# The first attention's loop over steps is unrolled into pairs on TensorE, VectorE and ScalarE

## The reference

```python
def swa_sink_attention(h, w_qkv, b_qkv, sinks, w_o, b_o):
    qkv = h @ w_qkv + b_qkv
    ...
    q = apply_rope(q, cos[:, None, None], sin[:, None, None]) * (A_HEAD_DIM ** -0.5)
    k = apply_rope(k, cos[:, None], sin[:, None])
    ...
    s = jnp.einsum('bnqkgd,bnskd->bnkgqs', qr, kb).astype(jnp.float32)
    p = sink_softmax(jnp.where(mask[:, None, None], s, NEG_INF), sink).astype(v.dtype)
    o_r = jnp.einsum('bnkgqs,bnskd->bnqkgd', p, vb).reshape(B, n_blk * BLOCK, A_Q_W)
```

## Time and profile before

| | us |
|---|---|
| median of three runs | 3612.8 (3612.68 to 3614.37) |
| the profiled execution | 3607.28 |
| its span | 3605.4 |
| PE busy over the span | 3241.1 (90%) |
| VectorE busy | 1766.6 (49%) |
| ScalarE busy | 1273.1 (35%) |
| GpSimd busy | 1849.1 (51%) |

### The profile page before, as it was taken

One profiled execution on the slowest core, in us unless ns is written; L12 is line 12 of the kernel. 1 busy time (PEld: TensorE's weight loads), 2 busy tenths in 40 slices (PEclk: granted clock), 3 DMA queues, 4 the chain that ended last, 5 costly groups with the idle time before them and its releaser, 6 DMA issues. The chain is left out here.

```text
span 3605.4 us, 57550 instructions
## 1 busy us (share of the span) xinstructions
PE 3241.1 (90%) x20001; PEld 2511.4 (70%) x20001; DVE 1766.6 (49%) x3672; ACT 1273.1 (35%) x2673; POOL 1849.1 (51%) x1443
## 2 busy tenths in 40 slices
PE   6999997896999995997999999999997996999960
PEld 4788885785888884996566666666655876888850
DVE  3555555676343334663554555455533663433316
ACT  2444444232232232443443444444342222223212
POOL 2555553343344432444789888888872223444412
PEclk8999998998999997998999999999998998999985
DMA  2011003543999965886121011022005448998817
GB/s 99 26 39 38 26 33 88 175 151 98 366 310 311 307 217 189 266 265 168 38 51 32 29 51 48 10 51 51 7 13 165 142 133 275 366 325 305 302 65 320
DMA packets 366625, 536.55 MB, mean 149 GB/s; under 512 B 91121, under 2 KB 286741, under 8 KB 359524
## 3 DMA queue, kind: packets, MB, share of 16 engines
q1 hardware_dynamic: 339460, 457.86, 39.7%
q0 software_dynamic: 26976, 76.27, 5.5%
HBM read 397.39 MB, written 145.38 MB: 151 GB/s over the span
## 5 line engine op out<-in xcount | busy, mean ns | idle before, releaser
L2039 POOL TENSOR_TENSOR ab_acc<-ab_acc,ab_pT 128x1024 f32<-128x1024 f32 (+2 forms) x320 | 654.2, 2044 | 136.7 <-ACT ab_pT L2073 102.4
L2073 ACT ACTIVATE ab_pT<-ab_S 128x512 f32<-128x512 f32 (+4 forms) x704 | 376.6, 537 | 576.1 <-PE ab_S L2147 359.7
L2089 DVE TENSOR_REDUCE ab_mx<-ab_W 128x2 f32<-128x1024 f32 (+5 forms) x352 | 347.0, 994 | 402.0 <-PE ab_W L2162 271.8
L1239 POOL DMA_INDIRECT scratch_y<-ex_y,ex_prow x64 | 64.7, 1011 | 491.2 <-issue 353.1
L2196 PE MATMUL ab_O<-ab_pT,ab_v 128*64 128x512 f32 (+4 forms) x1408 | 304.8, 549 | 0.0
L1409 PE MATMUL ex_G<-ex_xT,ex_wg 128*128 128x160 f32 x2048 | 293.4, 302 | 2.1 <-DMA ex_wu<-in_moe_w_up 2.1
L2145 PE MATMUL ab_S<-ab_q_hi,ab_k_hi 97*128 97x512 f32 (+3 forms) x704 | 292.7, 416 | 1.4 <-DVE ab_q_hi L2101 0.7
L1409 PE MATMUL ex_U<-ex_xT,ex_wu 128*128 128x160 f32 x2048 | 288.6, 299 | 0.0
L1409 PEld LDWEIGHTS ex_G<-ex_xT,ex_wg 128*128 128x128 f32 x2048 | 281.8, 191 | 7.3 <-issue 3.6
L1409 PEld LDWEIGHTS ex_U<-ex_xT,ex_wu 128*128 128x128 f32 x2048 | 281.7, 190 | 0.0
L1062 PE MATMUL pr_PR<-pr_wo_hi,pr_o_hi 128*128 128x512 f32 x528 | 218.6, 414 | 51.1 <-DVE pr_wo_lo L931 39.9
(11 more groups left out here) (308 smaller groups left out, 7106.6 us busy)
## 6 DMA issues: line engine op xcount, KB each, us to landing
ex_wg<-in_moe_w_gate SPq DMA_DIRECT2D x64, 1024.0 KB
ex_wu<-in_moe_w_up SPq DMA_DIRECT2D x64, 1024.0 KB
ex_wd<-in_moe_w_down SPq DMA_DIRECT2D x64, 1024.0 KB
pb_y<-scratch_y SPq DMA_DIRECT2D x17, 1024.0 KB
pr_o<-scratch_oT SPq DMA_DIRECT2D x33, 512.0 KB
scratch_h<-pr_h SPq DMA_DIRECT2D x33, 512.0 KB
scratch_xn<-pr_xn SPq DMA_DIRECT2D x33, 512.0 KB, 2.7
fi_y<-scratch_y SPq DMA_DIRECT2D x16, 1024.0 KB, 14.2
```

The source lines that it names most:

```text
L2039: nc.gpsimd.tensor_tensor(to, to, pT[0:r, U % RING, :, 0:n], ALU.add).then_inc(added, 1)
L2073: nc.scalar.activation(pT[0:r, U % RING, h, 0:n], S[0:r, h, 0:n], ACT.Exp, scale=B_SCALE).then_inc(exped, 1)
L2089: nc.vector.reduce_max(mx[:, :, t, c:c + 1].rearrange("p h a -> p (h a)"), W[:, j % 2, :, 0:n], AX.X).then_inc(emptied, 1)
```

## The change

The bodies of the steps become functions (score, turn, turn_meta, value on TensorE; hide, keep_p, keep_meta on VectorE; weigh, keep_p on ScalarE) with the same instructions and the same waits in each. The loops go over q in twos:

- TensorE: score q and q+1, job k, turn q-6 and q-5, job k+1, then (every second pair) turn_meta, then value q-8 and q-7 with the vmeta products behind a fourth. Value of an even step is thus one step later than before.
- VectorE: keep_o, hide q and q+1, denominators, job k, keep_p(q-6), job k+1, keep_meta.
- ScalarE: job k, weigh q and q+1, job k+1, square (now at k=4), keep_p(q-5).

Of a function whose body is that of the loop before, only the head stands here.

```diff
@@ ScalarE
+                def weigh(q):
...
+                def keep_p(u):
...
-                for q in range(NP + 6):
+                for q in range(0, NP + 6, 2):
                     n, k = divmod(q, PAIRS)
                     job(n, k)
...
-                    if k == 5 and live(n + 3):
+                    weigh(q)
+                    weigh(q + 1)
+                    job(n, k + 1)
+                    if k == 4 and live(n + 3):
                         square(n + 3)
+                    keep_p(q - 5)
@@ VectorE
-                for q in range(NP + 8):
+                def hide(q):
...
+                def keep_p(u):
...
+                def keep_meta(H):
+                    dve.wait_ge(flipped, 5 * H + 5)
+                    if H >= 2:
+                        dve.wait_ge(summed, 5 * (H - 2) + 5)
+                    nc.vector.tensor_copy(pmT[:, H % 2, :], PT[:, 0, 0:P]).then_inc(copied_dve, 1)
+
+                for q in range(0, NP + 9, 2):
                     n, k = divmod(q, PAIRS)
-                    if q % 4 == 3 and q >= 11:
-                        keep_o((q - 11) // 4)
...
+                    if q % 4 == 0 and q >= 12:
+                        keep_o((q - 12) // 4)
+                    hide(q)
+                    hide(q + 1)
                     if q % 4 == 0 and 4 <= q <= NP:
                         denominators(q // 4 - 1)
                     job(n, k)
...
+                    keep_p(q - 6)
+                    job(n, k + 1)
+                    if q % 4 == 0 and 8 <= q < NP + 8:
+                        keep_meta((q - 8) // 4)
@@ TensorE
-                for q in range(NP + 7):
+                def score(q):
...
+                def turn(u):
...
+                def turn_meta(H):
+                    pe.wait_ge(scaled, 3 * H + 3)
+                    pe.wait_ge(copied_dve, 3 * H + 2)
+                    nc.tensor.transpose(PT[:, 0, 0:P], pmeta[:, H % 2, :], ident[:, :]).then_inc(flipped, 1)
+
+                def value(u):
...
+                for q in range(0, NP + 8, 2):
+                    n, k = divmod(q, PAIRS)
+                    score(q)
+                    score(q + 1)
                     job(n, k)
...
+                    turn(q - 6)
+                    turn(q - 5)
+                    job(n, k + 1)
+                    if q % 4 == 0 and 8 <= q < NP + 8:
+                        turn_meta((q - 8) // 4)
+                    value(q - 8)
+                    value(q - 7)
```

More of the change, by code:

```diff
@@ L416, in _ @@
                         square(2)
-                for q in range(NP + 6):
+                def weigh(q):
+                    k = q % PAIRS
+                    if q >= NP:
+                        return
+                    H, i = divmod(q, 4)
+                    act.wait_ge(masked, q + 1)
+                    if q == 0:
+                        act.wait_ge(w_split, DC)
+                    if i == 0 and H >= 2:
+                        act.wait_ge(totalled, H - 1)
+                    if i == 0 and H >= 3:
+                        act.wait_ge(flipped, 5 * (H - 3) + 5)
+                    for g in range(2):
+                        last = nc.scalar.activation(prob[:, H % 3, i, g, :], z[:, q % 2, g, :], ACT.Exp, bias=negmax[:, H % 2, 2 * i + g:2 * i + g + 1],
+                                                    scale=-1.0, accum_out=psum_row[:, H % 2, 2 * i + g:2 * i + g + 1])
+                    last.then_inc(exped, 1)
+                    if i == 3:
+                        act.wait_ge(sink_in, H + 1)
+                        nc.scalar.activation(sexp[:, H % 2, :], sarg[:, H % 2, :], ACT.Exp).then_inc(sink_exped, 1)
@@ L419, in _ @@
+                def keep_p(u):
+                    if not 0 <= u < NP:
+                        return
+                    H, i = divmod(u, 4)
+                    act.wait_ge(flipped, flips(u))
+                    if u >= 3:
+                        act.wait_ge(summed, pv_count(u - 3))
+                    nc.scalar.copy(pT[:, u % 3, :], PT[:, 1, :]).then_inc(copied_act, 1)
+                for q in range(0, NP + 6, 2):
                     n, k = divmod(q, PAIRS)
                     job(n, k)
[L421 to L444, removed]
-                    if k == 5 and live(n + 3):
+                    weigh(q)
+                    weigh(q + 1)
@@ new lines, in hide @@
+                    if q >= NP:
+                        return
+                    H, i = divmod(q, 4)
+                    dve.wait_ge(scored, q + 1)
+                    if q >= 2:
+                        dve.wait_ge(exped, q - 1)
+                    for g in range(2):
+                        j = 2 * i + g
+                        last = nc.vector.tensor_tensor_reduce(out=z[:, q % 2, g, :], in0=S[:, q % 2, g, 0:BAND], in1=mask[:, min(n, 2), :],
+                                                              scale=-A_SCALE, scalar=negsinks[:, 2 * k + g:2 * k + g + 1], op0=ALU.add, op1=ALU.min,
+                                                              accum_out=negmax[:, H % 2, j:j + 1])
@@ new lines, in hide @@
+                    last.then_inc(masked, 1)
+                    if i == 3:
+                        dve.drain()
+                        nc.vector.tensor_tensor(sarg[:, H % 2, :], psinks[:, 8 * (H % 2):8 * (H % 2) + 8], negmax[:, H % 2, :], ALU.add).then_inc(sink_in, 1)
+                def keep_p(u):
+                    if not 0 <= u < NP:
+                        return
+                    H, i = divmod(u, 4)
+                    dve.wait_ge(flipped, flips(u))
+                    if u >= 3:
+                        dve.wait_ge(summed, pv_count(u - 3))
+                    nc.vector.tensor_copy(pT[:, u % 3, :], PT[:, 0, :]).then_inc(copied_dve, 1)
@@ L622, in _ @@
                         job(p, k)
-                for q in range(NP + 7):
+                def score(q):
                     n, k = divmod(q, PAIRS)
[L626 to L637, removed]
-                    job(n, k)
[L639 to L679, removed]
@@ new lines, in score @@
+                    if q >= NP:
+                        return
+                    if k == 0:
+                        pe.wait_ge(qk_low, 3 * n + 3)
+                        if n == 0:
+                            pe.wait_ge(zeroed, 1)
+                    if q >= 2:
+                        pe.wait_ge(masked, q - 1)
+                    for c, (qs, ks) in enumerate(((q_hi, k_hi), (q_hi, k_lo), (q_lo, k_hi))):
+                        for g in range(2):
+                            last = nc.tensor.matmul(S[:, q % 2, g, 0:BAND], qs[HD * g:HD * g + HD, n % 2, k, :], ks[HD * g:HD * g + HD, n % 4, :],
+                                                    start=(c == 0), stop=(c == 2))
@@ new lines, in score @@
+                    last.then_inc(scored, 1)
+                def turn(u):
+                    if not 0 <= u < NP:
+                        return
+                    H, i = divmod(u, 4)
+                    pe.wait_ge(scaled, 3 * H + 1 + i // 2)
+                    if i % 2 == 0 and u >= 2:
+                        pe.wait_ge(copied_dve, 3 * H + i // 2)
+                    if i % 2 == 1 and u >= 2:
+                        pe.wait_ge(copied_act, 2 * H + i // 2)
+                    for a in range(4):
+                        g, b = divmod(a, 2)
+                        last = nc.tensor.transpose(PT[:, i % 2, P * a:P * a + P], prob[:, H % 3, i, g, META + P * b:META + P * b + P], ident[:, :])
+                    last.then_inc(flipped, 1)
@@ new lines, in turn_meta @@
+                def turn_meta(H):
[3 more added lines that the diff above has]
+                def value(u):
+                    if not 0 <= u < NP:
+                        return
+                    H, i = divmod(u, 4)
+                    m = u // PAIRS
+                    if i % 2:
+                        pe.wait_ge(copied_act, 2 * H + i // 2 + 1)
+                    else:
+                        pe.wait_ge(copied_dve, 3 * H + i // 2 + 1)
+                    if i == 0 and H >= 1:
+                        pe.wait_ge(o_ready, H)
+                    for b in range(2):
+                        tile = max(m - 1 + b, 0)
+                        for g in range(2):
+                            last = nc.tensor.matmul(O[HD * g:HD * g + HD, P * i:P * i + P], v[:, tile, HD * g:HD * g + HD],
+                                                    pT[:, u % 3, P * (2 * g + b):P * (2 * g + b) + P],
+                                                    start=(i == 0 and b == 0), stop=False, skip_group_check=True)
+                    last.then_inc(summed, 1)
+                    if i == 3:
+                        if H == 0:
+                            pe.wait_ge(vm_ready, 16 * 8)
+                        pe.wait_ge(copied_dve, 3 * H + 3)
+                        for a in range(4):
+                            last = nc.tensor.matmul(O[:, P * a:P * a + P], vmeta[:, a, :], pmT[:, H % 2, :],
```

(2 more changed lines are left out.)

28 lines of the change are left out of this document (1 added, 27 removed).

## The result

The changed kernel takes 3640.41 us (median of four runs, 3639.68 to 3641.05) against 3612.74 of the kernel before (3609.65 to 3614.37): 1.0076 times the time, 95% interval 1.0061 to 1.0091, or 27.7 us more.

A forecast was written before the change was run, and what follows sets the result against it. TensorE, busy 32.20 of 32.20 us a tile, was taken to bound the kernel. Waits of 3.2 against 2.0 saved gave +1.2 a tile, +17 over tiles 1 to 14, +16 in all: 3612.8 + 16 = 3629, range 3608 to 3646.

The forecast's parts named there:

- The walk's own range: Whole kernel: 3621 to 3637 us, from 0.1 to 0.15 on each wait, 0.5 us a tile.
- the rival in which the runs don't merge: TensorE's score and value still pay 0.21 and 0.15 between two steps: some 15 us more, 3644; chance 0.09.
- The gain of merging: TensorE: merging saves 0.51 us a pair, 2.0 a tile; twelve scores take 0.93, sixteen value products 1.02.
- k=0,1: First pair of a tile: flip_x 1 waits 1.21 us for low behind both hides; 5.3 instead of 4.48.
- k=2,3 and k=4,5: Middle pairs of a tile: flip_q waits 0.23 us after each projection; 10.3 instead of 10.54, 9.4 instead of 9.56.
- k=6,7: Last pair of a tile: project 2 waits 1.3 us for lower_k behind hides and sink sum; 8.4 instead of 7.60.
- Turn_meta and the pair sums: Turn_meta costs 0.1 us more at k=0 and at k=4; the pairs together 33.4 against 32.2, +1.2 a tile.
- Tiles 15 and 16: Nothing is projected; merging saves half a microsecond a pair, turn_meta waits about as much for keep_p: 0 to -1 us.
- Tile 0: Start-up tile: nothing merges but score, and the same answers are waited for already: 0, within 1 us.
- the clock falls in the new waits: Rival: TensorE's granted clock drops in one such stretch in every tile, 40 us more, 3669; chance 0.04.
- From profile to median: Profiled execution 3607.28 us, with +16 3623.3; the median of the runs lies 5.5 above, so 3612.8 + 16 = 3629.
- the other queues: ScalarE, GpSimd and SyncE: their later exponentials, copies, scale and store were all taken at nothing.

The follow-up runs named there:

- e6: Changed kernel with k=0 step by step on all three engines, and at k=6 VectorE's lower_k and keep_p between the two hides: 3601.1 us, 0.9970 of before.
- e5: Changed kernel whose sink sum reads the sinks from a copy in PSUM, with a drain and the masks' signal behind it: 3632.5 us, 1.0055 of before.
- e8: The changed kernel once more, unaltered, for a second profile: 3641.9 us, one execution.
- e9: The kernel before the change once more, unaltered, for a second profile: 3608.2 us, one execution.
- e2: Changed kernel with only the sink sum of step 7 moved behind lower_k on VectorE: 3626.6 us, 1.0039 of before.
- e7: Kernel before the change, with the masking operations of hide at k=0 done twice on VectorE: 3634.6 us, 1.0061 of before.
- e4: Changed kernel with pairs kept at k=2 and k=4 only; k=0 and k=6 step by step on all three engines: 3603.6 us, 0.9978 of before.
- e1: Changed kernel with VectorE's job and keep_p ahead of the second hide at k=0 and k=6, ScalarE's high earlier at k=0: 3608.9 us, 0.9992 of before.
- e3: Changed kernel with TensorE's two values moved ahead of job k+1 as cover: 3618.8 us, 1.0023 of before.

## Why the prediction was right, step by step

The forecast was 3629, the range 3608 to 3646; 3640.4 came. The direction, the places and the reasons hold for tiles 1 to 14; the size, 16 us, was 28. The walk's own range, 3621 to 3637, missed it. The wider one holds it because its upper end was stretched to the rival in which the runs don't merge, and that rival did not come true; what fills the gap are other terms, listed below. That the range held is thus in part luck.

*The gain of merging*: right. 0.95 and 1.02 were forecast as 0.93 and 1.02. So the rival in which the runs don't merge falls.

*k=0,1*: right. Flip_x 1 at 3.47 (forecast 3.50), turn_meta at 4.16 (4.10), the pair 5.41 (5.3). Of the tenth between, 0.06 is turn_meta's later start and 0.02 value's behind it (0.23 after turn_meta, 0.21 before the change).

*k=2,3 and k=4,5*: right, 10.30 and 9.48 against 10.3 and 9.4. Flip_q comes 1.10 after the projection in both (298.04 to 299.14 in after, where the turn starts and where the flip does), and in e6 the same.

*k=6,7*: the mechanism right, the size not: 8.76 instead of 8.4. Project 2 starts at 3.58, not 3.26. The failed term is the sink sum, taken as 0.17 from the earlier trace rows. In after it takes 0.58 (first line of the VectorE fence) and ends at 304.12, just when a multiplication on GpSimd ends at 304.10:

```profile
301.73 2.37 POOL L324 TENSOR_TENSOR aa_qk<-aa_qk,aa_cs 128x1024 f32<-128x1024 f32 x1
```

This is so at the sum at k=7 of each of tiles 0 to 14 in after (0.54 to 0.58 us, and 1.22 in tile 0); all others take 0.17. Before, 2 of 34 were long. The row that I took the price from, 323.81 in the earlier trace rows, had missed GpSimd by 0.14 us, as GpSimd's own row of before shows:

```profile
321.28 2.39 POOL L351 TENSOR_TENSOR aa_qr<-aa_qk,aa_rot 128x1024 f32<-128x1024 f32 x1
```

It ends at 323.67. In the new order the sum starts in the middle of such an operation. With one operand in PSUM (e5) all 34 are short, though 15 of them start while GpSimd is in the middle of an operation, so what the sum waits for is SBUF, shared with GpSimd. The pair is 0.36 longer than forecast, 5 of the 12 us missed.

*Turn_meta and the pair sums*: a tenth each at k=0 and k=4 too little, 0.2 a tile, 3 us.

*Tiles 15 and 16*: wrong, forecast 0 to -1 together, measured +0.4: tile 15 +0.95, the rest of the stage -0.55. The term was turn_meta's wait, taken as about what a pair saves. TensorE in order of time in after, where the first of these falls:

```profile
585.07 0.30 PE L678 MATMUL aa_PT<-aa_ident,aa_pmeta 128*128 128x128 f32 x1 [1.55 <-DVE aa_pT L561]
...
594.78 0.30 PE L678 MATMUL aa_PT<-aa_ident,aa_pmeta 128*128 128x128 f32 x1 [1.46 <-DVE aa_pT L561]
```

With no job in between, nothing covers keep_p, which stands behind both hides: 1.5 us, twice in the tile, against four pairs at about 0.5: 3.0 - 2.0 = +1.0.

*Tile 0*: wrong, forecast 0 within 1, measured +2.8, of which the pair at k=0 has 0.6, k=2 0.6 and k=6 1.6. "The same answers are waited for already" was right, but the waits have grown, the sink sum is at its longest there (1.22 us), and the granted clock has fallen twice. Windows of 6 us with the columns of the earlier trace rows, of after, then e8, before and e9:

```profile
75.00:81.00 6.00, 4.49 (x25) 3.44 (x24) 4.29 (x17) 3.67 (x13) 1.39 (x4) 0.72 0.29 97
96.00:102.00 6.00, 4.22 (x28) 3.46 (x27) 4.58 (x13) 4.79 (x15) 5.72 (x4) 0.66 0.01 1
```

```profile
75.00:81.00 6.00, 5.85 (x28) 4.71 (x29) 2.64 (x11) 4.04 (x16) 0.00 (x0) 0.72 0.29 104
96.00:102.00 6.00, 3.89 (x23) 3.65 (x22) 3.46 (x11) 3.20 (x12) 5.48 (x5) 0.77 0.00 1
```

```profile
75.00:81.00 6.00, 5.17 (x28) 4.05 (x27) 2.06 (x9) 2.72 (x9) 0.00 (x0) 1.00 0.29 102
96.00:102.00 6.00, 5.35 (x48) 4.87 (x49) 4.74 (x13) 3.00 (x11) 5.35 (x7) 1.00 0.02 4
```

```profile
75.00:81.00 6.00, 4.45 (x24) 3.51 (x25) 3.03 (x10) 3.68 (x13) 0.46 (x1) 1.00 0.30 102
96.00:102.00 6.00, 5.02 (x47) 4.46 (x48) 4.16 (x10) 3.85 (x14) 5.62 (x6) 1.00 0.00 1
```

Both executions of after lost the clock in both places, and both of before kept it. The first place is flip_x 1 at k=0 and what follows it, the second the pair at k=6. TensorE in order of time, first after, then e8:

```profile
77.20 0.99 PE L597 MATMUL aa_PRJ<-aa_ident,aa_x 128*128 128x128 f32 x4 [1.51 <-DVE aa_x_lo L461]
...
97.88 1.91 PE L672 MATMUL aa_PT<-aa_ident,aa_prob 128*128 128x128 f32 x8
101.03 0.58 PE L611 MATMUL aa_PRJ<-aa_w_hi,aa_x_hi 128*128 128x256 f32 x1 [1.24 <-DVE aa_k_lo L489]
```

```profile
95.87 1.04 PE L672 MATMUL aa_PT<-aa_ident,aa_prob 128*128 128x128 f32 x8
99.01 0.45 PE L611 MATMUL aa_PRJ<-aa_w_hi,aa_x_hi 128*128 128x256 f32 x1 [2.11 <-DVE aa_k_lo L489]
```

The eight transposes take 1.04 or 1.91 and project 2 starts 3.15 later either way: VectorE sets that. In after the transposes are slow already, so there the clock had fallen ahead of the long wait; in e8 it fell behind it. In after project 2 comes 4.86 after its pair's first score (96.17), where before it was 3.86 (92.79 to 96.65). Then it starts slow: its first 16 matmuls take 3.59 us (101.03 to 104.62) against 2.02 before (96.65 to 98.67).

E2 tells the two causes apart. It has after's order but for the sum at step 7, and its one profile kept the clock at 1.00 from 74.5 us on, through tile 0, with the same wait ahead of the same flip:

```profile
77.50 0.66 PE L603 MATMUL aa_PRJ<-aa_ident,aa_x 128*128 128x128 f32 x4 [1.51 <-DVE aa_x_lo L461]
```

Its tile 0 takes 28.07, 3.55 less than in after: 1.3 because project 2 comes 3.55 after its score and not 4.86 (the sum is not ahead of it), 1.6 because its 24 matmuls take 3.06 and not 4.67, and 0.6 at k=0 and k=2 (3.76 and 9.00 against 4.05 and 9.34). So the clock costs some 2.2 in tile 0 and the sum 1.3; with neither, e2 is 0.8 shorter there than the kernel before.

So the rival "the clock falls in the new waits" has its mechanism in part, in two places of tile 0 and not in every tile: in all eleven profiles the clock was 1.00 from 106 to 550 us. E7 tries the first place by itself, with TensorE's order of before and only VectorE's work ahead of flip_x 1 made longer:

```profile
76.79 1.12 PE L578 MATMUL aa_PRJ<-aa_ident,aa_x 128*128 128x128 f32 x4 [1.49 <-DVE aa_x_lo L452]
```

Its clock fell right there, and twice more in the tile; the pairs at k=2 and k=4, whose instructions are those of before, hold 3.4 of its +5.1. Over the eleven profiles, the four in which this flip waited 0.83 (before, e4, e6, e9) kept the clock at it, and of the seven in which it waited 1.40 to 1.51 four lost it (after, e5, e7, e8) and three did not (e1, e2, e3). The longer wait thus goes with the fall but does not settle it; what decides is open. The Trainium skill, "TensorE: Matmul & The Clock Gate", Part 1, holds that an idle TensorE falls back to half its clock. The levels agree (in after the clock was 0.50 from 97.9 to 104.6), but TensorE was not idle through the stretch ahead of that: it was busy 5.32 us of the 6.80 from 91.0 to 97.8.

*From profile to median*: the forecast carried the +16 over to the median, the profile of before lying 5.5 under it; that of after lies 0.4 under its own. Had I compared the two profiles, I would have read +32.7.

The miss of 12 us is thus made of terms that were sized too small: k=6 (0.36 x 14 = 5.0), the tenths at k=0 and k=4 (2.8), tile 0 (2.8) and the tiles behind (0.4 for -0.5, 0.9), 11.5 together. Of the other queues, taken at nothing, none has TensorE waiting for it in tiles 1 to 14, but GpSimd's work is what makes the sink sum long, and so has its part in the 5.0.

## What to carry to other kernels

Merging steps to save the cost of changing form pays only where the job between them is long enough to cover the answers; look for the shortest steps (here k=0 and k=6) and leave those apart, or put what the next job waits for ahead of the other work in the answering engine's order. List for each wait what now stands ahead of the awaited instruction on its engine, in the start-up too, where a longer wait can cost clock besides. Before summing durations of a moved instruction, look at what the engine that shares its memory does at the new time: one row of it is not its price.

## What the runs showed of the hardware that I had not expected

An add of 8 elements per partition took up to 2.13 us on VectorE (e4, at k=7 of fourteen tiles), where its usual time is 0.17. VectorE and GpSimd in e1, in order of time:

```profile
322.15 1.90 DVE L555 TENSOR_TENSOR aa_sarg<-aa_psinks,aa_negmax 128x8 f32<-128x8 f32 x1
```

```profile
321.63 2.39 POOL L351 TENSOR_TENSOR aa_qr<-aa_qk,aa_rot 128x1024 f32<-128x1024 f32 x1
```

The sum ends at 324.05, GpSimd's operation at 324.02. In e1 30 of the 34 sums took 1.10 us or more, and the pairs show no cost: at k=6 lower_k stands ahead of the sum, and the pairs at k=2 stayed at 10.31. In before, after, e1, e3, e4 and e6 each of the long sums ended 0.02 to 0.03 us after an operation of GpSimd. The Trainium skill, "SBUF — State Buffer", SBUF: two separate sides, says that a VectorE operation with two SBUF inputs and a GpSimd operation that reads SBUF exclude each other, and that the one that starts second waits for the whole of the other; these rows and e5 agree. VectorE's masked operation of hide, whose large operands are one in PSUM and one in SBUF, kept its 0.49 to 0.50 in all 272 places of both after and e1, though 125 and 146 of them overlapped GpSimd's work.
